# Depthwise convolution in 8 phases of 16 channels, with a quarter of its shift matrices built on GpSimd, in an 8-core encoder block

## What is computed

```python
proj = n @ w_in                                  # 2*1024 GLU, 1024 pool, 2*2048 gate columns
gate_a, gate_b = sigmoid(...), sigmoid(...)
a, g = split(glu_in); a = a * sigmoid(g)         # 1024 channels
a = depthwise_conv(a, conv_w, K=31, causal) + conv_b
a = silu(layer_norm(a, ln_a_g, ln_a_b))
y_a = a @ w_a_out + b_a_out
y_b = (grouped (mean_pool(v, w) - v) @ w_b_group + b_b_group) * ls_b     # windows w = 2, 4, 8, 16
h = h + ada_gate * ((gate_a * y_a + gate_b * y_b) @ w_out)
```

## Time and profile before

| | us |
|---|---|
| median of 3 runs | 2600.87 (2597.87 to 2666.51) |
| the profiled execution: its time | 2596.2 |
| its span, slowest core (3) | 2594.6 |
| spans of the 8 cores | 2586.4 to 2594.6 |
| mean granted TensorE clock of the cores | 0.991 to 0.996 of 2.4 GHz |

### The profile page before, as it was taken

One profiled execution on the slowest core, in us unless ns is written; L12 is line 12 of the kernel. 1 busy time (PEld: TensorE's weight loads), 2 busy tenths in 40 slices (PEclk: granted clock), 3 DMA queues, 4 the chain that ended last, 5 costly groups with the idle time before them and its releaser, 6 DMA issues.

```text
span 2594.6 us, 38158 instructions; the slowest of 8 cores (2586.4 to 2594.6 us)
## 1 busy us (share of the span) xinstructions
PE 2499.8 (96%) x14726; PEld 1405.4 (54%) x14726; DVE 1023.2 (39%) x1487; ACT 429.3 (17%) x772; POOL 336.9 (13%) x605
## 2 busy tenths in 40 slices
PE   1999999999999999999999999999999999999997
PEld 0566666666666666677544444444444444444445
DVE  5467555444454546646832224610021100211026
ACT  3422000100000012523511111510000000000013
POOL 1220111111111110000111100000000000000034
PEclk9999999999999999999999999999999999999999
DMA  9999999899998984843385452454444445444435
GB/s 232 159 165 197 193 171 154 148 159 159 162 154 139 166 153 99 183 89 70 68 188 94 77 108 47 82 98 80 71 80 79 73 74 82 75 73 81 68 63 167
DMA packets 103888, 310.05 MB, mean 119 GB/s; under 512 B 11808, under 2 KB 26528, under 8 KB 103584
## 3 DMA queue, kind: packets, MB, share of 16 engines
q0 software_dynamic: 79024, 260.12, 60.9%
q1 hardware_dynamic: 24688, 47.50, 5.6%
HBM read 546.09 MB, written 16.78 MB: 217 GB/s over the span
## 4 chain that ended last, share of the span: by engine, by line
PE 91%; DMA 5%; ACT 1%; DVE 1%; issue 1%; POOL 0%; DVEq 0%; SPq 0%; ACTq 0%; POOLq 0%
PE ps L275 91%; DMA ring<-w_head 2%; DMA ring<-w_ada 1%; ACT nT L285 1%; DMA hT<-xT 1%; DMA ring<-w_out 1%; DVE U L289 1%; DVE rs L306 0%; DVE hT L300 0%; ACT L285 0%; POOL ring L322 0%; ACT rs L285 0%; DVE rs L289 0%; SPq L337 0%; ACTq L1107 0%
## 5 line engine op out<-in xcount | busy, mean ns | idle before, releaser
L275 PE MATMUL ps<-nT,ring 128*128 128x352 bf16 (+3 forms) x9344 | 1650.3, 339 | 15.0 <-DMA ring<-w_head 8.2
L275 PEld LDWEIGHTS ps<-nT,ring 128*128 128x128 bf16 x9344 | 914.0, 98 | 737.9 <-issue 22.5
L275 PE MATMUL ps<-U,ring 128*128 128x352 bf16 (+3 forms) x4480 | 794.7, 339 | 3.1 <-DMA ring<-w_out 3.1
L275 PEld LDWEIGHTS ps<-U,ring 128*128 128x128 bf16 x4480 | 435.9, 98 | 355.9 <-issue 5.0
L285 ACT ACTIVATE tmp<-ps 128x512 f32<-128x512 f32 (+1 forms) x268 | 142.7, 535 | 1708.8 <-PE ps L275 1678.4
L289 DVE TENSOR_TENSOR U<-tmp,ps 128x352 bf16<-128x352 f32 (+1 forms) x190 | 113.1, 598 | 769.0 <-PE ps L275 759.1
L300 DVE SCALAR_TENSOR_TENSOR hT<-ps,ghT,hT 128x352 f32<-128x352 f32 (+3 forms) x288 | 182.8, 636 | 355.7 <-PE ps L275 355.7
L322 POOL DMA_DIRECT2D ring<-w_in x212 | 112.5, 532 | 1189.8 <-PE ps L275 1175.4
L385 DVE SCALAR_TENSOR_TENSOR ring<-ring,rs 128x2048 bf16<-128x2048 bf16 x112 | 253.0, 2286 | 13.6 <-DMA ring<-w_adaD 13.6
L322 POOL DMA_DIRECT2D ring<-w_out x118 | 62.8, 533 | 507.0 <-PE ps L275 498.0
L285 ACT ACTIVATE nT<-hT 128x512 bf16<-128x512 f32 (+4 forms) x138 | 79.1, 582 | 183.7 <-DVE hT L300 174.0
(11 more groups left out here) (67 smaller groups left out, 592.3 us busy)
## 6 DMA issues: line engine op xcount, KB each, us to landing
ring<-w_in POOLq DMA_DIRECT2D x212, 512.0 KB, 6.6
ring<-w_adaD POOLq DMA_DIRECT2D x112, 512.0 KB, 9.9
ring<-w_out POOLq DMA_DIRECT2D x80, 512.0 KB, 5.5
hT<-xT SPq DMA_DIRECT2D x8, 2112.0 KB, 23.6
ring<-w_ada POOLq DMA_DIRECT2D x32, 512.0 KB, 18.5
ring<-w_out POOLq DMA_DIRECT2D x38, 384.0 KB, 6.1
hscr<-hT SPq DMA_DIRECT2D x16, 512.0 KB, 12.9
hT<-hscr SPq DMA_DIRECT2D x16, 512.0 KB, 13.2
```

The source lines that it names most:

```text
L275: e.matmul(o, l, r, start=st, stop=sp, skip_group_check=sk),
```

## The change

NPH becomes 8: a block holds 16 channels x 8 phases, there are 64 blocks of 128 columns, and the 31 taps need NM = 5 shift matrices. On the partitions, phase now runs fastest (channel x 8 + phase). The projection steps keep their column blocks. What follows from it:
- `build_w` has 8 blocks for each chunk, into 8 buffers; every fourth (`blk % 4 == 3`) is a GpSimd instruction, the others stay on VectorE. The tap values come by two DMAs.
- `conv` puts four blocks in a PSUM bank instead of two, and evicts each with two activations of 128 columns.
- `to_phase` makes 8 DMAs for each chunk (16 partitions to 128) and `from_phase` likewise, called at the end of each `ln_apply(c)`, from SP for even c and from POOL for odd c.
- `ln_stats` adds up four parts instead of two; `ln_apply` has 8 activations per chunk.
- The five waiting sigmoids stand after `ln_apply(3)` instead of after `pool_dve(6)`.

```diff
-C_ID = 433
-NPP = 465
-NPH = 4
+C_ID = 529
+C_PQ = 545
+NPP = 553
+NPH = 8
 OWN = TOWN // NPH
-NM = 9
+NM = 5
+NWB = 8
+CWA = 52
...
-        Bcw = uview(7408, 1, NBLK * NM * NPH, BF16)
+        Bcws = (uview(7408, 1, CWA * NM * NPH, BF16), uview(12288, 1, (NBLK - CWA) * NM * NPH, BF16))
-        Bw = uview(8448, 5, NM * P, BF16)
-        Bsq = uview(8448 + 2880, 2, 2 * OWN, F32)
+        Bw = uview(8448, NWB, NM * P, BF16)
+        Bsq = uview(8448 + 2560, 2, 512, F32)
...
-        TB4 = [(0, HALO + OWN)] + [(HALO + q * OWN, HALO + (q + 1) * OWN) for q in range(1, NPH)]
+        TB4 = [(0, HALO + 256)] + [(HALO + q * 256, HALO + (q + 1) * 256) for q in range(1, 4)]
...
             def to_phase(c0, c1):
+                for c in range(c0, c1):
+                    for j in range(NPH):
+                        S.add("sp", lambda e, o=Bx4.ap3[:, NPH * c + j, :], i=Babf.ap3[j * CHB:(j + 1) * CHB, c, :]:
+                              e.dma_start(out=o, in_=i),
+                              reads=[Babf.r(c)], writes=[Bx4.rr(NPH * c, NPH * c + NPH)], dma=("xi", c))
+
+            def from_phase(c):
+                eng = "sp" if c % 2 == 0 else "pool"
                 for j in range(NPH):
+                    S.add(eng, lambda e, o=Bz.ap3[j * CHB:(j + 1) * CHB, c, :], i=Bz4.ap3[:, NPH * c + j, :]:
+                          e.dma_start(out=o, in_=i),
+                          reads=[Bz4.rr(NPH * c, NPH * c + NPH)], writes=[Bz.r(c)], dma=("zo", c))
...
             def build_w(c):
                 for blk in range(NPH * c, NPH * c + NPH):
-                    wb = blk % 5
+                    wb = blk % NWB
+                    Bc, b0 = (Bcws[0], blk) if blk < CWA else (Bcws[1], blk - CWA)
                     n = NM * NPH
-                    op_tt(Bw.ap3[:, wb, :].rearrange("p (a b) -> p a b", a=n),
-                          id32[:].unsqueeze(1).to_broadcast([P, n, CHB]),
-                          Bcw.ap3[:, 0, blk * n:(blk + 1) * n].unsqueeze(2).to_broadcast([P, n, CHB]), ALU.mult,
-                          [("id32", 0, 1), Bcw.r(0, blk * n, (blk + 1) * n)], [Bw.r(wb)])
+                    op_tt(Bw.ap3[:, wb, :].rearrange("p (m c q) -> p m c q", m=NM, q=NPH),
+                          id32[:].unsqueeze(1).unsqueeze(3).to_broadcast([P, NM, CHB, NPH]),
+                          Bc.ap3[:, 0, b0 * n:(b0 + 1) * n].rearrange("p (m q) -> p m q", m=NM).unsqueeze(2).to_broadcast(
+                              [P, NM, CHB, NPH]), ALU.mult,
+                          [("id32", 0, 1), Bc.r(0, b0 * n, (b0 + 1) * n)], [Bw.r(wb)], eng="pool" if blk % 4 == 3 else "dve")
...
                 for pr in range(2 * c, 2 * c + 2):
                     bk = new_bank()
-                    for i in range(2):
-                        blk = 2 * pr + i
-                        wb = blk % 5
+                    for i in range(4):
+                        blk = 4 * pr + i
+                        wb = blk % NWB
...
-                op_tt(rs[:, 0:256], rs[:, 0:256], rs[:, 256:512], ALU.add, [Brs.r(0, 0, 512)], [Brs.r(0, 0, 256)])
-                op_tt(rs[:, 256:512], mu, rl, ALU.add, [MU_R, RL_R], [Brs.r(0, 256, 512)])
+                for w in (256, 128):
+                    for o in (0, 512):
+                        op_tt(rs[:, o:o + w], rs[:, o:o + w], rs[:, o + w:o + 2 * w], ALU.add,
+                              [Brs.r(0, o, o + 2 * w)], [Brs.r(0, o, o + w)])
+                op_copy(rs[:, 128:256], rs[:, 512:640], [Brs.r(0, 512, 640)], [Brs.r(0, 128, 256)])
                 bk = new_bank()
-                op_mm(psum[bk][:, :], oblk[:], rs[:, 0:512], True, True,
+                op_mm(psum[bk][:, 0:256], oblk[:], rs[:, 0:256], True, True,
...
-            for c in range(4):
+            for c in range(8):
                 ln_apply(c)
-            from_phase(0, 4, range(NPH), "sp")
-            for c in range(4, 8):
-                ln_apply(c)
-            from_phase(4, 8, (0, 1), "sp")
-            from_phase(4, 8, (2, 3), "pool")
+                if c == 3:
+                    for f in sigs:
+                        f()
             pool_dve(6)
-            for f in sigs:
-                f()
             pool_mm(7, sl_pool)
```

More of the change, by code:

```diff
@@ L35 @@
 C_CB = 337
-C_LG = 369
-C_LB = 401
-C_ID = 433
-NPP = 465
-NPH = 4
+C_LG = 401
+C_LB = 465
+C_ID = 529
+C_PQ = 545
+NPP = 553
+NPH = 8
 OWN = TOWN // NPH
@@ L343, in build_nc @@
         op_memset(ones_rms[:], 1.0 / D, [("ones_rms", 0, 1)])
-        op_memset(oblk[:], 0.0, [("oblk", 0, 1)])
-        for q in range(NPH):
-            op_memset(oblk[q * CHB:(q + 1) * CHB, q * CHB:(q + 1) * CHB], 1.0 / WC, [("oblk", 0, 1)])
         op_copy(id32[:], pp[:, C_ID:C_ID + CHB], [Bpp.r(0, C_ID, C_ID + CHB)], [("id32", 0, 1)])
+        op_ts(oblk[:].rearrange("p (c q) -> p c q", q=NPH), pp[:, C_PQ:C_PQ + NPH].unsqueeze(1).to_broadcast([P, CHB, NPH]),
+              1.0 / WC, None, ALU.mult, None, [Bpp.r(0, C_PQ, C_PQ + NPH)], [("oblk", 0, 1)])
         op_act(scb[:], pp[:, C_C:C_C + KC], AF.Silu, [Bpp.r(0, C_C, C_C + KC)], [("scb", 0, 1)])
@@ L580, in build_nc @@
         HM_R = Bpp.r(0, C_HM, C_HM + 1)
-        TB4 = [(0, HALO + OWN)] + [(HALO + q * OWN, HALO + (q + 1) * OWN) for q in range(1, NPH)]
+        TB4 = [(0, HALO + 256)] + [(HALO + q * 256, HALO + (q + 1) * 256) for q in range(1, 4)]
         def mixer():
             halves = [(0, 512), (512, 1024)]
[L585 to L589, removed]
+            for i, Bc in enumerate(Bcws):
+                lo = i * CWA * NM * NPH
+                S.add("pool", lambda e, o=Bc.ap3[:, 0, :], i=cwp[:, lo:lo + Bc.width]: e.dma_start(
+                    out=o, in_=i, max_dma_last_dim=8192), writes=[Bc.r(0)], dma="cw" if i == 0 else "cw2")
@@ L591, in to_phase @@
             def to_phase(c0, c1):
-                for j in range(NPH):
[L593 to L605, removed]
+                for c in range(c0, c1):
[3 more added lines that the diff above has]
+                              reads=[Babf.r(c)], writes=[Bx4.rr(NPH * c, NPH * c + NPH)], dma=("xi", c))
@@ L655, in conv @@
                     if pr == 1:
-                        op_tt(acc_s, yv[:, 0:512], yv[:, 512:1024], ALU.add, [By.rr(0, 4)], [Brs.r(0, 0, 512)])
+                        op_tt(acc_s, yv[:, 0:512], yv[:, 512:1024], ALU.add, [By.rr(0, 8)], [Brs.r(0, 0, 512)])
                         op_tt(acc_q, Bsq.ap3[:, 0, :], Bsq.ap3[:, 1, :], ALU.add, [Bsq.rr(0, 2)], [Brs.r(0, 512, 1024)])
@@ L680, in pool_dve @@
                 cur = 0
-                for lvl, U0 in zip(range(g + 1), (4, 5, 6, 8)):
+                for lvl, U0 in zip(range(g + 1), (1, 2, 3, 4)):
                     nxt = 1 if cur != 1 else 2
                     o, i = V[nxt], V[cur]
-                    if lvl < 2:
-                        sh = 1 << lvl
+                    sh = 1 << lvl
+                    if sh < NPH:
                         op_tt(o[:, sh:NPH, U0:PHW], i[:, sh:NPH, U0:PHW], i[:, 0:NPH - sh, U0:PHW], ALU.add,
@@ L690, in pool_dve @@
                     else:
-                        sh = 1 << (lvl - 2)
-                        op_tt(o[:, :, U0:PHW], i[:, :, U0:PHW], i[:, :, U0 - sh:PHW - sh], ALU.add,
+                        op_tt(o[:, :, U0:PHW], i[:, :, U0:PHW], i[:, :, U0 - 1:PHW - 1], ALU.add,
                               [Bv.r(cur)], [Bv.r(nxt)])
@@ L1184, in _prep_inputs @@
     }
[L1185 removed]
+    cwz = np.zeros((CHB, NPH, NBLK, NM, NPH), dtype=np.float32)
     for p in range(NPH):
@@ L1190, in _prep_inputs @@
                 if 0 <= k < 31:
-                    cwz[p, :, :, m, q] = conv_w[k].reshape(NBLK, CHB).T
+                    cwz[:, p, :, m, q] = conv_w[k].reshape(NBLK, CHB).T
     shared["cwp"] = cwz.reshape(P, NBLK * NM * NPH)
     def ph(v):
-        return np.tile(np.asarray(v, dtype=np.float32).reshape(NBLK, CHB).T, (NPH, 1))
+        return np.repeat(np.asarray(v, dtype=np.float32).reshape(NBLK, CHB).T, NPH, axis=0)
     in_maps = []
@@ L1222, in _prep_inputs @@
                 cnt = min(i + 1, wdw) if ch == 0 else wdw
-                ppv[:, C_CNT + g * 16 + (i % NPH) * 4 + i // NPH] = np.float32(1.0) / np.float32(cnt)
-        ppv[:, C_ID:C_ID + CHB] = np.tile(np.eye(CHB, dtype=np.float32), (NPH, 1))
+                ppv[:, C_CNT + g * 16 + (i % NPH) * (16 // NPH) + i // NPH] = np.float32(1.0) / np.float32(cnt)
+        ppv[:, C_ID:C_ID + CHB] = np.repeat(np.eye(CHB, dtype=np.float32), NPH, axis=0)
+        ppv[:, C_PQ:C_PQ + NPH] = np.tile(np.eye(NPH, dtype=np.float32), (CHB, 1))
         m = {"xT": np.ascontiguousarray(xs[PERM].T), "pp": ppv,
```

19 lines of the change are left out of this document (10 added, 9 removed).

## The result

The changed kernel took 2667.68 us (median of 4 runs, 2666.99 to 2667.95) against 2599.37 before: a ratio of 1.027, 95% interval 1.0257 to 1.0282. Forecast were 2661, 2638 to 2700.

What follows compares the result with a forecast made beforehand. TensorE, busy 96% of the span, was taken to bound the kernel. Conv columns -13.5, seven stalls +71 and the middle +2.5 sum to +60 us: 2656 for the profiled execution, 2661 for the median, range 2638 to 2700.

Steps and rivals of the forecast that it cites:

- The mechanism: After conv 0 to 6 TensorE waits for weight fills queued behind GpSimd's two builds: seven times, 71 us together.
- The conv columns: Conv matmuls: 320 of 128 columns at 56.3 ns instead of 288 at 109.4 ns, a gain of 13.5 us.
- The 81 ns of the Trainium skill: Conv matmuls, rival: load and matmul pairs of 128 columns take about 81 ns, gain 5.6 us; chance 0.2.
- The builds: GpSimd at each conv: two builds of 1.9 us each, ending 5.5 us after the conv's start.
- The quiet row: GpSimd's quiet two-input products: 1.93 ns an element, so 1.4 us a build, kept as lower end.
- The landing: Weight fill behind the builds: 5.3 us from issue to landing, TensorE resuming at 10.8, a wait of 8.5 us.
- The clock: TensorE after each of seven stalls: fallen clock costs 1.6 us each, lower end 0, upper 3.
- The middle: From the last conv into the output loop: statistics, normalising activations and return copies cost +2.5 us, between 0 and 8.
- not held: Rival, steps after the convs: fills don't stand behind GpSimd's waiting multiply; only -13.5 and the middle remain, 2590 us; chance 0.05.

## Why the prediction held, and where its terms were off

- **The mechanism was right**, and so was the place: seven waits, each behind a conv, each behind GpSimd's two builds, ended by the landing of a weight fill. Three experiments carry it: the builds off GpSimd, the fills ahead of them, and one such build in the old kernel.
- **The conv columns** were right to the tenth: 40 matmuls in 2.25 us, 56.3 ns each, a gain of 13.5 us. The 81 ns of the Trainium skill (TensorE: Matmul & The Clock Gate, Back-to-back issue gap) does not hold here; a weight load for every 128 columns stays hidden.
- **The builds were overpriced**: 1.24 us each (2.47 for two) and not 1.9. The quiet row was the nearer one, 1.4. The reason given for 1.9, that VectorE builds its six matrices at that moment, was wrong: VectorE's builds stand behind its adding up, which waits for ScalarE's evictions. On core 4, with conv 5 starting at 1269.32:

```profile
1270.77 2.50 POOL L292 TENSOR_TENSOR U<-id,U 128x640 bf16<-128x640 bf16 x2 [24.50 <-PE ps L278]
...
1276.07 4.50 DVE L292 TENSOR_TENSOR U<-id,U 128x640 bf16<-128x640 bf16 x6
```

  GpSimd's began 1.51 us after conv 0, and the fills were issued at 3.93; over the seven stalls at 4.2 in the mean, instead of 5.5, since the two builds took 2.91 and 2.80 us where they ran beside a mean pool (conv 4 and 6), and 1.36 us passed ahead of the fill behind conv 3.
- **The landing was underpriced**: on core 4 from issue to TensorE's restart 7.0, 8.1, 7.9, 7.4, 8.4, 6.3 and 7.1 us, 7.4 in the mean, against 5.3. On core 7 it was 5.3 to 6.1. The two errors, -1.3 and +2.1 a stall, cancel in good part: a wait of 9.2 us on the slowest core (7.6 on core 7) for 8.5. That the time came out within 7 us is partly luck. Why the landing is longer, and longer on some cores, isn't settled. The old conv with its larger copies had 6.8 as well, so the small copies aren't needed for it. That several cores now ask for weights in bursts at one time was not tried.
- **The clock** cost 2.0 us a stall and not 1.6: after 8 to 10 us idle it is low from the first matmul on, where after 3 us it fell only on the way.
- **The middle** was +6 and not +2.5. The activations were priced well (12.44 us for 32, 0.39 each; two more table loads), in the timeline of ScalarE:

```profile
1329.03 12.44 ACT L288 ACTIVATE hT<-hT,pp_sb 128x128 bf16<-128x128 f32 x32
1341.48 1.28 ACT L288 ACT_TABLE_LOAD   x1
...
1346.65 12.43 ACT L288 ACTIVATE hT<-hT,pp_sb 128x128 bf16<-128x128 f32 x32
```

  But the sums came 2.1 us later than before, not 1; the clock fell behind this wait, which cost 1.4 us, where the prediction had charged the clock for the seven stalls alone; and the last copies took up to 6.3 us to land instead of the 2.5 of the earlier trace rows, among the reloads of 512 KB behind them.
- **The step that failed** is in the rival "not held": 2590 if the fills were free. It counted only the columns and the middle, and so took for granted that VectorE's builds stay hidden under TensorE's steps, while TensorE's conv became 1.7 us shorter and the builds 0.8 us longer. With the fills free the kernel stands at 2599.5 us, the median of both experiments that free them: VectorE's queue is the next bound. The forecast didn't feel it, because seven long waits hid it.

## What to carry to other kernels

A queue that fetches weights lives by its lead: an instruction that waits for TensorE, put ahead of a fetch, makes the fetch's whole lead worth nothing, however short the instruction is. Ask of each new instruction on such a queue what it waits for and what stands behind it, and write the fetches first. When a long wait is taken away, look at once for the engine that it had let catch up, and when copies are issued sooner, for the bulk that then starts among them.

## What the runs showed that was not expected

- GpSimd and VectorE slow each other when a GpSimd product runs beside VectorE's fp32 operations on two SBUF inputs: 3.75 us for 2.47, and 6.45 for 4.72. Single instructions look like turns taken and not like a shared rate: VectorE's first operation kept its 1.10 us while the build beside it took 2.48 instead of 1.25, then VectorE's second took 1.17 instead of 0.30 and its third 1.84 instead of 0.97. How builds on both engines would get on isn't shown: in no trace did they run side by side for more than 0.4 us.
- Copies of 32 KB between parts of SBUF took 2.1 us to land alone and 5.8 to 8.5 among fills of 512 KB.
- Ahead of the fill at 1223.94, GpSimd stood 1.36 us for nothing that the profile shows, at the same place of the program on the other cores. Its cause is open.
